# Four value pages on four column groups in the sample's attention

## The reference, cut to what matters

```python
def diff_attn_sample(q, k_new, v_new, k_past, v_past, lam):
    ...
    w = diff_combine(jnp.concatenate([s_past, s_new], axis=-1), lam).astype(v_new.dtype)
    return (jnp.einsum('bhqs,bshe->bqhe', w[..., :P], v_past)
            + jnp.einsum('bhqs,bshe->bqhe', w[..., P:], v_new))
```

## Time and profile before

| | us |
|---|---|
| median of 3 runs | 1536.34 (1535.75 to 1539.92) |
| the profiled execution, first to last instruction (span) | 1536.8 |
| TensorE busy | 1397.7 (91%) |
| VectorE busy | 856.5 (56%) |
| ScalarE busy | 534.2 (35%) |
| products with the values, L756, 256 matmul instructions | 127.9 busy |

### The profile page before, as it was taken

How to read it: one execution, slowest core, us unless ns; L and a number is a source line. 1 busy time by engine, 2 the same in 40 slices (tenths; PEclk the granted TensorE clock), 3 DMA queues, 4 the chain that set the end, 5 groups by cost and what they waited for, 6 DMA issues and landing times.

```text
span 1536.8 us, 19072 instructions
## 1 busy us (share of the span) xinstructions
PE 1397.7 (91%) x7054; PEld 968.0 (63%) x7054; DVE 856.5 (56%) x1097; ACT 534.2 (35%) x613; POOL 21.2 (1%) x26
## 2 busy tenths in 40 slices
PE   5999899999999988999877898888898999999986
PEld 1583735788888885498322222228355888888864
DVE  1435463666666622554797999655705666656434
ACT  0331213555555512343111111123215555555321
POOL 2000010000000000000000000000100000000000
PEclk9999999999999998999877788798857999999988
DMA  9927440899999874354438987865104999999400
GB/s 337 365 92 266 165 164 0 294 342 341 335 337 337 307 286 154 125 184 153 151 109 314 328 314 273 314 226 195 60 0 163 341 336 343 341 339 339 149 2 28
DMA packets 143712, 355.36 MB, mean 231 GB/s; under 512 B 4706, under 2 KB 4899, under 8 KB 143652
## 3 DMA queue, kind: packets, MB, share of 16 engines
q1 hardware_dynamic: 142388, 350.97, 63.9%
q0 software_dynamic: 1264, 3.59, 0.7%
HBM read 351.27 MB, written 3.28 MB: 231 GB/s over the span
## 4 chain that ended last, share of the span: by engine, by line
PE 77%; DVE 15%; issue 3%; ACT 2%; DMA 1%; SPq 0%; ACTq 0%; POOL 0%; DVEq 0%
PE pj L372 27%; PE gu L590 23%; PE pj L609 15%; DVE wring L1763 4%; PE pj L756 3%; DVE tokB L1766 3%; PE tb L403 3%; PE tb L406 3%; PE gu L438 3%; PE pj L383 1%; DMA wring<-in_ada_w 1%; DVE xT L1435 1%; DVE yT L1433 1%; DVE rs L1432 1%; ACT reg L1069 1%
## 5 line engine op out<-in xcount | busy, mean ns | idle before, releaser
L1618 DVE TENSOR_TENSOR wlo<-wring,whi 128x2048 fp32r<-128x2048 f32 x128 | 290.1, 2288 | 102.2 <-ACT whi L1173 102.1
L1173 ACT ACTIVATE whi<-wring 128x2048 fp32r<-128x2048 f32 x128 | 245.0, 1918 | 140.4 <-PE gu L590 140.4
L609 PEld LDWEIGHTS pj<-tokB,wring 128*128 128x128 f32 x2048 | 233.5, 192 | 4.7 <-issue 2.1
L609 PE MATMUL pj<-tokB,wring 128*128 128x128 f32 x2048 | 234.0, 275 | 1.7 <-issue 1.7
L590 PE MATMUL gu<-whi,xhi 128*128 128x512 f32 x512 | 205.9, 402 | 13.2 <-DVE xlo L1644 13.2
L1069 ACT ACTIVATE reg<-pj 128x264 f32<-128x264 f32 (+4 forms) x166 | 83.2, 507 | 380.0 <-PE pj L372 209.7
L590 PE MATMUL gu<-wlo,xhi 128*128 128x512 f32 x512 | 203.5, 398 | 0.0
L590 PE MATMUL gu<-whi,xlo 128*128 128x512 f32 x512 | 201.9, 394 | 0.0
L372 PE MATMUL pj<-wring,cT 128*9 128x512 f32 x384 | 175.6, 612 | 5.4 <-DMA wring<-in_ada_w 4.6
L756 PE MATMUL pj<-wring,ws 128*8 128x512 f32 x256 | 127.9, 659 | 6.4 <-DMA wring<-in_cache_v 5.4
L590 PEld LDWEIGHTS gu<-whi,xhi 128*128 128x128 f32 x512 | 98.1, 192 | 35.0 <-DVE xlo L1644 8.2
(11 more groups left out here) (281 smaller groups left out, 1652.1 us busy)
## 6 DMA issues: line engine op xcount, KB each, us to landing
wring<-in_moe_w_gate SPq DMA_DIRECT2D x32, 2048.0 KB, 9.5
wring<-in_moe_w_up SPq DMA_DIRECT2D x32, 2048.0 KB, 10.3
wring<-in_moe_w_down SPq DMA_DIRECT2D x32, 2048.0 KB, 9.9
wring<-in_ada_w SPq DMA_DIRECT2D x24, 2048.0 KB, 10.4
wring<-in_cache_k SPq DMA_DIRECT2D x64, 512.0 KB, 5.0
wring<-in_cache_v SPq DMA_DIRECT2D x64, 512.0 KB, 4.9
wring<-in_a_w_in SPq DMA_DIRECT2D x4, 2048.0 KB, 19.8
wring<-in_a_w_out SPq DMA_DIRECT2D x2, 2048.0 KB, 15.3
```

Source lines behind the costliest of these rows:

```text
L609: m = pe.matmul(bank[:, i * P:(i + 1) * P], w[:, k, f * P:(f + 1) * P], aT[:, k, :], start=(k == 0), stop=(k == FB - 1))
L1173: act.activation(whi[q], quarter(wring, q, s), ACT.Copy).then_inc(hi_ready, 1)
L1618: dve.tensor_tensor(quarter(wlo, q, s), quarter(wring, q, s), whi[q].bitcast(F32), ALU.subtract).then_inc(lo_ready, 1)
```

## The change

- `values` puts page p of a group of four on its own 32 partitions of the bank, rows 32p to 32p + 7, so that each page uses another quarter of the columns of the array; each quarter accumulates its two pages (k = 0 and 1).
- ScalarE evacuates all 128 partitions of the bank.
- The pick is a matmul per head: the stationary operand is the evacuated 128 x 128 block, the moving one a single column of a new constant `group_sum` (ones on rows 32g + h), so that it adds the four groups and selects the head's row. VectorE copies 8 adjacent columns.
- VectorE clears the four banks `pj` at the start, and TensorE waits for that before its first `group`.
- The 128 columns of ones become one column, broadcast with stride 0 wherever it is used (`ones()`); `kst` shrinks from 1037 to 919 columns.

```diff
+NG = 4
+QUAD = P // NG
+K_ID, K_ROT, K_TRI, K_MASK, K_IOTA, K_PART = 0, 128, 256, 384, 640, 640 + T
+K_SUM = K_PART + 5
+K_ONE = K_SUM + NR
+K_N = K_ONE + 1
...
-    k[:, K_ONE:K_ONE + P] = 1.0
+    k[:, K_ONE] = 1.0
+    for g in range(NG):
+
+        k[QUAD * g:QUAD * g + NR, K_SUM:K_SUM + NR] = np.eye(NR)
...
+        group_sum = kst[:, K_SUM:K_SUM + NR]
+
+        def ones(a=0, b=P, n=P):
+
+            return kst[a:b, K_ONE:K_ONE + 1].to_broadcast([b - a, n])
...
                 k = banks[0]
                 banks[0] += 1
+                if k == 0:
+
+                    pe.wait_ge(banks_clear, 1)
...
-                    m = pe.matmul(st[which][:, :], kst[:, K_ONE:K_ONE + P], src[:, k, :],
+                    m = pe.matmul(st[which][:, :], ones(), src[:, k, :],
...
-                    out = pj[(banks[0] + n) % NBANK][0:H, :]
-                    for p in range(4):
-                        m = pe.matmul(out, sW[:, s, 4 * k + p, :], wring[:, slot, p * D + n * 512:p * D + (n + 1) * 512],
-                                      start=(k == 0 and p == 0), stop=(k == 1 and p == 3))
+                    bank = pj[(banks[0] + n) % NBANK]
+                    for p in range(NG):
+
+                        m = pe.matmul(bank[QUAD * p:QUAD * p + H, :], sW[:, s, 4 * k + p, :],
+                                      wring[:, slot, p * D + n * 512:p * D + (n + 1) * 512], start=(k == 0), stop=(k == 1))
...
-                    small([((P, H * c, H), tr(osb[0:H, c * P:(c + 1) * P], H)) for c in range(C)])
+                    small([((P, c, 1), mm(osb[:, c * P:(c + 1) * P], group_sum[:, c:c + 1])) for c in range(C)])
...
-                        evac(osb[0:H, n * 512:(n + 1) * 512], rows=H, n=512)
+                        evac_wide(osb[:, n * 512:(n + 1) * 512], P)
...
+            for bank in pj:
+                i = dve.memset(bank[:, :], 0.0)
+            i.then_inc(banks_clear, 1)
             dve.memset(pos[:], 0.0)
...
-                                          batch()[:, 0:(H + 1) * (H - 1) + 1:H + 1].unsqueeze(2)))
+                                          batch()[:, 0:H].unsqueeze(2)))
```

More of the change, by code:

```diff
@@ L68 @@
 LOADS = [("k", 0), ("k", 1)] + [x for m in range(NB - 2) for x in (("k", m + 2), ("v", m))] + [("v", NB - 2), ("v", NB - 1)]
-K_ID, K_ROT, K_ONE, K_TRI, K_MASK, K_IOTA, K_PART = 0, 128, 256, 384, 512, 768, 768 + T
-K_N = 768 + T + 5
+NG = 4
[4 more added lines that the diff above has]
+K_N = K_ONE + 1
 V_LNG, V_LNB, V_AG, V_AB, V_SUB, V_N = 0, 32, 64, 72, 80, 81
@@ L332, in build @@
         routed = sem("routed")
+        banks_clear = sem("banks_clear")
         more = [{n: sem(f"more{l}_{n}") for n in ("x", "piece", "done", "silu", "evac", "mask")} for l in range(DEPTH)]
@@ L546, in moe @@
                 tiles = (P, P, NB)
-                small([((NE, 0, 1), mm(key[0:n, j, :], kst[0:n, K_ONE:K_ONE + 1], j == 0, j == 2))
+                small([((NE, 0, 1), mm(key[0:n, j, :], ones(0, n, 1), j == 0, j == 2))
                        for j, n in enumerate(tiles)])
@@ L557, in moe @@
                     for i in range(j):
-                        parts.append((at_j, mm(kst[:, K_ONE:K_ONE + n], key[:, i, :], False, False)))
+                        parts.append((at_j, mm(ones(n=n), key[:, i, :], False, False)))
                     parts.append((at_j, mm(kst[0:n, K_TRI:K_TRI + n], key[0:n, j, :], False, True)))
@@ L723, in _ @@
             for c in range(2):
-                small([((P, 0, 64), mm(kst[HD * c:HD * (c + 1), K_ONE:K_ONE + P], rs[HD * c:HD * (c + 1), 0:64]))])
+                small([((P, 0, 64), mm(ones(HD * c, HD * (c + 1)), rs[HD * c:HD * (c + 1), 0:64]))])
             operand()
-            small([((P, 0, 1), mm(kst[0:1, K_ONE:K_ONE + P], lams[0:1, 4:5]))])
+            small([((P, 0, 1), mm(ones(0, 1), lams[0:1, 4:5]))])
             to_tokens(uT)
@@ L803, in _ @@
                     for h in range(H):
-                        small([((P, 0, TP), mm(kst[:, K_ONE:K_ONE + P], sqT[:, h, 0:TP]))])
+                        small([((P, 0, TP), mm(ones(), sqT[:, h, 0:TP]))])
                     at["rms"] = b.n
@@ L807, in _ @@
                     operand()
-                    small([((P, 0, 16), mm(kst[:, K_ONE:K_ONE + P], smx[:, 16 * (s - 1):16 * s]))])
+                    small([((P, 0, 16), mm(ones(), smx[:, 16 * (s - 1):16 * s]))])
                 if s < NB:
@@ L825, in _ @@
             squares()
-            small([((P, 0, H * NB), mm(kst[:, K_ONE:K_ONE + P], sqT[:, :, TP:T]))])
+            small([((P, 0, H * NB), mm(ones(), sqT[:, :, TP:T]))])
             at["rms_sample"] = b.n
```

## The result

The changed kernel takes 1545.74 us (median of 8 runs, 1542.61 to 1551.50) beside 1536.77 for the kernel before (8 runs): 1.0050 times, interval 1.0031 to 1.0070.

What follows compares the result with a forecast made beforehand. VectorE was taken to bound the attention turns, with TensorE mostly hidden. The terms -4.4 + 14.7 + 0.5 - 4.0 + 0.4 - 1.0 - 0.2 = +6.0 us, put on the median, gave 1542.3, range 1531 to 1548.

Steps and rivals of the forecast that it cites:

- Turn 2: First run of values takes less time, so VectorE's waits of 3.2 and 1.9 us shrink: -4.4 us, bounds 0 and -5.1.
- half overlap: Products with the values on column groups run two at a time (factor 2); with the long pick, 1542.3 us, chance 0.42.
- rival of full overlap: Values run four at a time; turn 2 saves 5.1, turns 7 and 8 5.3; +4.0 us, 1540.3, chance 0.13.
- The picks: Turns 2 to 6: the longer pick is paid on VectorE's path, 4 x 3.0 + 2.7 = +14.7 us.
- +0.5 behind them: TensorE's `spread` and prompt scores behind the picks make VectorE wait in turn 3 only: +0.5 us.
- the choice on which the sign hung: Clock at the picks taken as 0.50, 3.0 us more each; at full clock 1.3 each, not slower, chance 0.25.
- Turns 7 and 8: `values(6)` starts 3.0 later but ends at 1000.7 instead of 1004.7, pick of turn 7 included: -4.0 us.
- the pick of turn 8: Clock high behind the tile: pick costs 1.3 us more, VectorE's own chain covers 0.9: +0.4 us.
- -1.0 in turn 9: Only VectorE's 1.0 us wait at L1394 goes, the reciprocal covering the rest: -1.0 us.
- the -0.2 of the start: Loading 118 fewer columns of constants, 60 KB, at the kernel's start: -0.2 us, an upper estimate.

Runs made afterwards that it cites:

- experiments 1 and 2: Kernel before with only the pick changed to eight float32 products: 1550.28 us, 1.0075; changed kernel with the pick as eight transposes, group sum left out: 1531.22 us, 0.9948.
- early pick: Changed kernel with the pick of turns 2 to 7 moved right behind the values, its reader behind the turn's last scores: 1530.39 us, 0.9947.
- old layout: Constants padded to their old width, so later buffers lie as before: changed kernel 1541.78 us, 1.0028; with the early pick 1529.16 and 1528.23 us, 0.9935 and 0.9945.
- early_36_again: Repeat of the changed kernel with early pick, old layout and three idle transposes behind each pick of turns 2 to 7: 1526.25 us, 0.9926.

## Why the prediction was right

The forecast was 1542.3 in a range of 1531 to 1548, slower with a chance of 0.50; it came to 1545.74, slower by 0.5%. Its main mechanism is what happened: VectorE pays for the pick, at the low clock. The overlap was mis-sized, and costs outside the attention are missing from the sum.

- **Turn 2**: -4.4 predicted, with half overlap. Both waits are gone, 3.2 and 1.9, which is the -5.1 of the rival of full overlap. VectorE came into the turn 0.6 us later (824.46 instead of 823.82 at the read of the broadcast maxima, L1807, now L1828), so its L1847 (now L1868) comes 4.6 sooner (838.56 instead of 843.20). That this is near the -4.4 is chance.
- **The picks**: +14.7 for turns 2 to 6 and +0.5 behind them; by the waits it is +14.3, and 1.0 behind them. All six picks take 3.54 (3.6 predicted), and at the reader of turn 6 the kernel is 10.7 us late where the sum had -0.2 - 4.4 + 14.7 + 0.5 = 10.6, with small errors that cancel. That the low clock would hold there was the choice on which the sign hung; experiments 1 and 2 show both of its halves. The Trainium skill (TensorE: Matmul & The Clock Gate, LDWEIGHTS) has 107 ns for such a load and names no clock; 3.54 us for 16 are 221 ns at 0.50, so the measurement decides against the rule there, while at full clock 1.93 for 16, 121 ns, is near it.
- **Overlap**: the step that failed. "I take 2", on the argument that the two instructions of a float32 product on one group cannot lie beside each other; it is 3.8. How the instructions of the four pages interleave to give it, the rows don't show. The Trainium skill (the same page, Part 3: Packing small matmuls) speaks of 2.38 times for three column tiles; no run here has three. That the time of one page's product is about all that four need, the trace bears out: one page is four instructions, 3.4 us at the low clock, and the four pages take 3.60.
- **Turns 7 and 8**: -4.0 predicted with the tile of L801 not binding. Because of the almost full overlap `values(6)` ends early (1008.5) and TensorE waits 1.7 us for the tile, which was issued at 999.90: its landing binds, and the turns give back 10.7 - 5.4 = 5.3, the -5.3 of the rival of full overlap.
- **The rest of the attention**: +0.4 for the pick of turn 8 (measured 0.3), -1.0 in turn 9 (measured -1.05, no wait at L1412, the reciprocal still 12.94 us). From the first value to L1412 that makes 4.8, where the sum, without the -0.2 of the start, has 6.2 and the rival of full overlap 4.2.
- **What was missing**: costs outside the attention, 2.5 us in the spans. The smaller `kst` stood in the sum only as a shorter load (-0.2); that it moves all buffers behind it and slows the experts' products by 3.3 us isn't in it, nor that 128 more instructions bring a stop of 2.1 us onto the tail. Of these 5.4 us, 3.2 are offset in the two stretches that were not explained, and 0.3 come on top ahead of the first expert. So the forecast came out near the time partly because an error in the overlap and the missing costs have opposite signs.

## What to carry to other kernels

Here an edit that took some 74 us of busy time off a hidden engine (products with the values, 127.9 to 53.4) and put 17.6 us of waiting on the bounding one lost. Look for the place where nothing waits for the new work, as with the early pick: it turned +0.5% into -0.5%, and -0.5 to -0.7% with the old layout. Price the work of TensorE beside a bound engine at the clock that the row next to it will have after the change, not before. And when an edit changes the size of a buffer or the number of instructions, compare the stages that were not touched too, before a difference is put down to the edit's own mechanism.

## What was not expected of the hardware

- Four float32 products on four column groups ran 3.8 times as fast as one behind the other: 16 instructions of 512 columns in 3.60 us at clock 0.50, and at clock 1.00 32 in 3.62, where they took 13.90 before. The latter is `values(7)` of early_36_again, the second kernel with 36 idle instructions:

```profile
1010.82 3.62 PE L774 MATMUL pj<-wring,ws 128*8 128x512 f32 x32
```

- Behind a longer wait, TensorE's next work ran slower. In early_36_again, TensorE waits 6.6 us for the tile after the shorter values, and then the tile takes 9.43 us; after the change, behind a wait of 1.7, it takes 7.04 (shown above, at clock 1.00). The rows of early_36_again, its timeline and then its clock:

```profile
993.72 9.43 PE L389 MATMUL pj<-wring,cT 128*9 128x512 f32 x16 [6.63 <-DMA wring<-in_ada_w]
```

```profile
993.70:1003.20 9.50, 9.48 (x17) 1.75 (x18) 0.00 (x0) 0.00 (x0) 0.00 (x0) 0.74 1.05 386
```

- A shift of buffers in SBUF by 480 bytes made the experts' products 2 to 4 ns longer (of some 390), by 448 bytes 3 to 7.
- A stop of 2.2 to 2.7 us on TensorE without a wait appears or vanishes at one place with the number of its instructions before it.
